# Where the fourth layer's modulation tiles are computed, and in which order the halved layers begin

## The reference, cut to what matters

```
sh1, sc1, gt1, sh2, sc2, gt2 = split(silu(c) @ w_ada[l] + b_ada[l], 6)     # for c and for c_ctx
h = rmsnorm(x, g2[l]) * (1 + sc2) + sh2
a, b = split(h @ w_up[l], 2)                                              # 2816 features each
x = x + gt2 * ((silu(a) * b) @ w_down[l])                                 # layers 0 and 1
x = x + gt2 * ((silu(dwconv3(a)) * b) @ w_down[l])                        # layers 2 and 3
```

## Time and profile before

| | |
|---|---|
| median of 3 runs | 3387.64 us (3385.45 to 3387.78) |
| the profiled execution's own time | 3385.83 us |
| its span | 3384.5 us |
| PE busy | 3247.7 us, 96% |
| VectorE (DVE) busy | 2159.3 us, 64% |
| FFN of layer 0, 1, 2, 3, about | 455 to 950, 1515 to 1862, 2218 to 2740, 2995 to 3375 us |

### The profile page before, as it was taken

One profiled execution on the slowest core, in us unless ns is written; L12 is line 12 of the kernel. 1 busy time (PEld: TensorE's weight loads), 2 busy tenths in 40 slices (PEclk: granted clock), 3 DMA queues, 4 the chain that ended last, 5 costly groups with the idle time before them and its releaser, 6 DMA issues. The chain is left out here.

```text
span 3384.5 us, 45127 instructions
## 1 busy us (share of the span) xinstructions
PE 3247.7 (96%) x17822; PEld 2767.8 (82%) x17822; DVE 2159.3 (64%) x3582; ACT 1404.8 (42%) x2261; POOL 223.0 (7%) x336
## 2 busy tenths in 40 slices
PE   6998999999999999999999999989999999999998
PEld 4787789999978888878888886889888987678887
DVE  4677477888765554558657466487888855654444
ACT  4567363333444334342223345363333443542333
POOL 0001100000010000003001000100000010010001
PEclk9999999999999999999999999999999999999999
DMA  5500123444221221215544211123444231123232
GB/s 216 216 23 2 38 77 123 132 143 137 87 90 50 96 77 50 90 69 195 173 148 156 84 45 51 44 86 116 140 127 129 87 99 57 44 83 99 90 101 83
DMA packets 98689, 334.39 MB, mean 99 GB/s; under 512 B 11872, under 2 KB 16768, under 8 KB 95024
## 3 DMA queue, kind: packets, MB, share of 16 engines
q1 hardware_dynamic: 77072, 252.63, 22.2%
q0 software_dynamic: 21408, 78.88, 7.4%
HBM read 329.37 MB, written 2.10 MB: 98 GB/s over the span
## 5 line engine op out<-in xcount | busy, mean ns | idle before, releaser
L1184 ACT ACTIVATE WH<-WR 128x1024 fp32r<-128x1024 f32 (+3 forms) x520 | 445.8, 859 | 1019.4 <-PE PS L586 749.1
L1797 DVE TENSOR_TENSOR WL<-WR,WH 128x1024 fp32r<-128x1024 f32 (+3 forms) x520 | 509.6, 981 | 478.6 <-ACT WH L1184 476.8
L586 PE MATMUL PS<-HH,WH 128*128 128x512 f32 (+1 forms) x1544 | 526.7, 373 | 10.7 <-DVE WL L1797 8.4
L586 PE MATMUL PS<-HH,WL 128*128 128x512 f32 (+1 forms) x1544 | 522.0, 370 | 0.0
L586 PE MATMUL PS<-HL,WH 128*128 128x512 f32 (+1 forms) x1544 | 521.7, 370 | 0.0
L586 PE MATMUL PS<-D,WH 128*128 128x512 f32 x1648 | 421.4, 361 | 0.3 <-DVE D L2244 0.2
L586 PEld LDWEIGHTS PS<-HH,WH 128*128 128x128 f32 x1544 | 270.0, 188 | 71.3 <-DVE WL L1797 12.9
L586 PEld LDWEIGHTS PS<-D,WH 128*128 128x128 f32 x1648 | 275.5, 188 | 52.5 <-DVE D L2244 2.0
L586 PEld LDWEIGHTS PS<-HL,WH 128*128 128x128 f32 x1544 | 268.9, 188 | 51.0 <-issue 1.0
L586 PEld LDWEIGHTS PS<-HH,WL 128*128 128x128 f32 x1544 | 269.2, 188 | 50.6
L586 PE MATMUL PS<-D,WL 128*128 128x512 f32 (+1 forms) x824 | 257.2, 360 | 0.0
(11 more groups left out here) (369 smaller groups left out, 6100.6 us busy)
## 6 DMA issues: line engine op xcount, KB each, us to landing
WR<-in_win SPq DMA_DIRECT2D x176, 512.0 KB, 3.5
AT<-in_adat POOLq DMA_DIRECT2D x144, 512.0 KB, 3.9
WR<-in_wret SPq DMA_DIRECT2D x64, 512.0 KB, 3.7
WR<-in_zin SPq DMA_DIRECT2D x36, 512.0 KB, 3.5
WR<-in_wdn SPq DMA_DIRECT2D x32, 448.0 KB, 3.4
WR<-in_wdn SPq DMA_DIRECT2D x48, 256.0 KB, 2.9
WR<-in_wdn SPq DMA_DIRECT2D x32, 320.0 KB, 2.9
AR<-in_ada SPq DMA_DIRECT2D x8, 1024.0 KB, 9.7
```

The source lines that it names most:

```text
L586: mm = PE.matmul(dst[:, a:b], w(u)[:, k * P:(k + 1) * P], h[:, k, a:b], start=(k == 0 and i == 0), stop=(k == nk - 1 and i == 2))
L1184: AC.activation(M.hi(u), M.raw(u), COPY).then_inc(*on.up("w_hi", u))
L1797: VE.tensor_tensor(M.lo(u), M.raw(u), M.hi(u).bitcast(F32), ALU.subtract).then_inc(*on.up("w_lo", u))
```

## The change

1. Tiles. The slots are now given by the FFN f in which they lie. FFN 1 gets the 48 tiles of layer 2 and the first 32 tiles of layer 3 (16 wide, 16 narrow). In its first two chunks a pair carries three tiles (the last pair of the chunk two) and each down product one; in the third chunk a pair carries three tiles, one wide and two narrow ones, and a down product none. All 48 of layer 2's tiles are of two instructions each. FFN 2 keeps 16 narrow tiles, all of them beside down products. In FFN 0 the two tiles of pairs 3 and 4 both stand beside pair 4.
2. Begin of the halved layers. The second sum of activation blocks has a place of its own (X2, where CB and the sums of weights lie), so `turned_low(1)` no longer has to follow `turned(3)`. On ACT `turned_high(0)` goes ahead of the refill of the fourth unit and `turned_high(3)` one half product later. On DVE `turned(3)`, `turned_low(0)`, `turned_low(3)` and the sums 7 and 3 of weights go behind the first refills of halves.
3. The convolution's steps in layer 2's halves. `conv_high` and `conv_low` of a pair go to the step behind product 1 of the pair after the next, and in the chunk's last pair behind product 2; `conv_multiply` goes from the step behind product 2 to the one behind product 5.

```diff
+EARLY = [(3, v) for v in range(32)]
+MORE = (6, 6, 8)
...
+        self.top = wide
+        self.X2 = t("X2", [P, 4, Q])
...
+def ada_slots(f):
     at = {}
+    wide, narrow = [(f + 1, v) for v in range(2 * KT)], [(f + 1, v) for v in range(2 * KT, NV)]
+    if f == 1:
+        wide = iter(wide + EARLY[:2 * KT])
+        narrow = iter(narrow + EARLY[2 * KT:])
+        for ch, nj in enumerate(CHUNKS[f]):
             for j in range(nj):
+                at["up", ch, j] = (next(wide), *(next(narrow) for _ in range(1 + (j < MORE[ch]))))
+            for m in range(KT if ch < 2 else 0):
+                at["down", ch, m] = (next(wide) if m < 5 else next(narrow),)
         return at
+    if f == 2:
+        narrow = [t for t in wide + narrow if t not in EARLY]
+    wide, narrow = iter(wide), iter(narrow)
+    for ch, nj in enumerate(CHUNKS[f]):
+        for j in range(nj):
+            if f == 0:
+                n = (2 if j == 4 else 0) if ch == 0 else 1 + (ch < 4 and j in (1, 2))
+            else:
+                n = 0
...
@@ ScalarE, halves
+            if l > 0 and i == 1 and j > js[1]:
+                conv_high(j - 2)
             if i in (1, 5, 6) or i == 3 and l > 0:
                 keep(j, i)
+            if l > 0 and i == 2 and j == js[-1]:
+                conv_high(j - 1)
...
-            if ch == 0 and q == 1:
+            if ch == 0 and q == 2:
                 turned_high(l, 3)
...
-                if i == (4 if j == js[-1] else 5) and j > js[0]:
-                    conv_high(j - 1)
@@ ScalarE, feed_forward
                 if l in HALVED and jj == 0:
                     whole(f"{l}b", l, [(1, k) for k in range(0 if l < 2 else 4, KT)])
+                    turned_high(l, 0)
                 refill(W.after(u, 4 if l in HALVED and jj else 3))
...
                     turned_high(l, 1)
                     turned_high(l, 2)
-                    turned_high(l, 0)
@@ VectorE, halves
+            if l > 0 and i == 1 and j > js[1]:
+                conv_low(j - 2)
+            if l > 0 and i == 2 and j == js[-1]:
+                conv_low(j - 1)
...
+            if ch == 0 and q == 0:
+                turned_low(l, 0)
             if ch == 0 and q == 1:
+                turned(l, 3)
+            if ch == 0 and q == 3:
                 turned_low(l, 3)
...
-                if i == (4 if j == js[-1] else 5) and j > js[0]:
-                    conv_low(j - 1)
...
-                if i == 2 and j > js[0]:
+                if i == 5 and j > js[0]:
                     conv_multiply(j - 1)
-            if i == 1 and (ch or j > js[0]):
+            if i == 1:
                 weight_sum(up + 2 * j, 3)
@@ VectorE, feed_forward
-                if l in HALVED and jj == 1:
-                    turned_low(l, 2)
-                    turned_low(l, 0)
                 refill(W.after(u, 2))
                 if l in HALVED and jj == 1:
                     refill(W.after(u, 3))
+                    turned_low(l, 2)
+                    weight_sum(up + 4, 7)
...
                         turned(l, 1)
                         turned(l, 2)
-                        turned(l, 3)
...
                 if l in HALVED and jj == 0:
-                    for i in (5, 6, 7, 3):
-                        weight_sum(up + 4, i)
+                    weight_sum(up + 4, 5)
+                    weight_sum(up + 4, 6)
                     turned_low(l, 1)
@@ GpSimd
+        for n in range(len(ada_order(l))):
+            modulation(l, n)
```

More of the change, by code:

```diff
@@ L539, in ada_columns @@
     return (0, 1) if l in (0, 2) or v < 2 * KT else (0,)
-def ada_slots(l):
+def ada_slots(f):
     at = {}
-    if l - 1 not in HALVED:
-        v = 0
-        for ch, nj in enumerate(CHUNKS[l - 1]):
-            for j in range(nj):
[L550 to L554, removed]
-        return at
[L556 to L559, removed]
-        for m in range(0 if ch else 1, KT - 2 if ch < 4 else 0):
-            at["down", ch, m] = (next(wide if ch == 0 or m in (1, 3, 4, 5)[4 - WIDE_DOWN[ch]:] else narrow),)
-    return at
@@ new lines, in ada_slots @@
+    if f == 2:
[7 more added lines that the diff above has]
+                n = 0
+            tiles = tuple(t for t in (next(narrow, None) for _ in range(n)) if t)
+            if tiles:
+                at["up", ch, j] = tiles
+        for m in range(0 if ch else 1, KT - 2 if ch < 4 else 0):
+            if f == 0 and (ch == 0 or m in (1, 3, 4, 5)[4 - WIDE_DOWN[ch]:]):
+                at["down", ch, m] = (next(wide),)
+            else:
+                tile = next(narrow, None)
+                if tile:
+                    at["down", ch, m] = (tile,)
@@ L570, in tensor_program, with ada_order @@
+    return at
+def ada_order(f):
+    return list(sum(ada_slots(f).values(), ()))
 def tensor_program(PE, M, on, FIRST):
@@ L1327, in turned_high @@
         else:
[L1328 removed]
+            dst, src = M.XH[:, n], M.X2[:, :, :] if n == 1 else M.XF[:, n]
         AC.activation(dst, src, COPY).then_inc(*on.up("t_hi", (l, n)))
@@ L1818, in scales, with ada_tiles @@
         step(i, ("scl", l, part))
[L1820 to L1824, removed]
+    def ada_tiles(f, tiles):
+        order = ada_order(f)
+        for l, v in tiles:
+            n = order.index((l, v))
             AT, cols = M.AT[n % 2], ada_columns(l, v)
@@ L1827, in ada_tiles @@
             if n:
-                VE.wait_ge(*on("ada_taken", (l, order[n - 1])))
+                VE.wait_ge(*on("ada_taken", order[n - 1]))
             for j in cols:
@@ L1834, in ada_bias @@
     def ada_bias(l):
-        VE.wait_ge(*on("ada_taken", (l, ada_order(l)[-1])))
+        VE.wait_ge(*on("ada_taken", ada_order(l - 1)[-1]))
         for j in range(2):
@@ L2083, in halves @@
         js, order, segs = range(plain(l, ch), nj), halves_order(l, ch), segments(l)
-        slots = ada_slots(ada)
+        slots = ada_slots(l)
         def ahead(n):
@@ L2183, in halves @@
             if i == 1 and ("up", ch, j) in slots:
-                if ch == 0 and j == js[1]:
+                if ch == 0:
                     VE.wait_ge(*on("cb", ada))
-                ada_tiles(ada, slots["up", ch, j])
+                ada_tiles(l, slots["up", ch, j])
         j = js[-1]
@@ L2202, in feed_forward @@
         n = segs[-1][1]
-        slots = ada_slots(ada) if ada is not None else {}
+        slots = ada_slots(l) if ada is not None else {}
         for ch, nj in enumerate(CHUNKS[l]):
@@ L2269, in feed_forward @@
                 if ada is not None:
-                    ada_tiles(ada, slots.get(("down", ch, m), ()))
+                    ada_tiles(l, slots.get(("down", ch, m), ()))
                 if ada is not None and ch == LAST[l] and m == 0:
@@ L2702, in squares, with modulation @@
             done = event
-    def modulation(l, n):
-        order = ada_order(l)
+    def modulation(f, n):
+        order = ada_order(f)
         if n == 0:
-            PO.dma_start(flat(M.CB, 0, 2), dram["cb"][min(l // 2, 1)]).then_inc(*on.up("cb_load", l, 16))
-        if n >= NV:
-            return
+            PO.dma_start(flat(M.CB, 0, 2), dram["cb"][min((f + 1) // 2, 1)]).then_inc(*on.up("cb_load", f + 1, 16))
         if n > 1:
-            PO.wait_ge(*on("ada_taken", (l, order[n - 2])))
-        PO.dma_start(M.AT[n % 2][:, :], dram["adat"][l - 1, order[n]]).then_inc(*on.up(f"mod_load{n % 2}", (l, order[n]), 16))
+            PO.wait_ge(*on("ada_taken", order[n - 2]))
+        l, v = order[n]
+        PO.dma_start(M.AT[n % 2][:, :], dram["adat"][l - 1, v]).then_inc(*on.up(f"mod_load{n % 2}", (l, v), 16))
     def feed_forward(l):
         PO.wait_ge(*(on("t_lo", (l, 3)) if l in HALVED else on("h_lo", (f"{l}b", 1, KT - 1))))
-        for n in range(NV):
-            modulation(l + 1, n)
+        for n in range(len(ada_order(l))):
+            modulation(l, n)
     def context_square(k):
@@ L2756, in pool_program @@
     squares("1b", S)
-    for n in range(NV):
-        modulation(2, n)
+    for n in range(len(ada_order(1))):
+        modulation(1, n)
         if 8 <= n < 16:
```

16 lines of the change are left out of this document (7 added, 9 removed).

## The result

The changed kernel takes 3400.95 us (median of 5 runs, 3398.43 to 3403.05), the kernel before 3385.86 us beside it: a ratio of 1.0044 with a 95% interval of 1.0031 to 1.0057. It is slower by 15 us, and the forecast of 3385 with its range up to 3396 was wrong. The span of the profiled execution is 3397.1 us, 12.6 more than before: the three changed FFNs are 16.2 us longer in it, and the stages between them, where the change does nothing, came 3.6 shorter.

What follows compares the result with a forecast made beforehand. PE, busy for 96% of the span, was taken as the bound, leaving about 137 us of idle time to win. The terms -17.1 + 16.6 - 2.0 + 0.3 = -2.2 us gave 3385 us, range 3371 to 3396.

Steps and rivals of the forecast that it cites:

- FFN 2's chunks: Fewer tiles and moved convolution steps: 3.9 us won in each of three chunks, 4.5 last, 0.9 first; 17.1 us together.
- bound of 10: FFN 2: only 10 us won if the moved steps make ACT's keep of product 1 late in each pair.
- two late spots: Last pair of FFN 2's chunks: join 7 about 0.6 us late, and 1.4 us idle before the down products.
- the 2 beside POOL: FFN 1's first chunk: 2 us more lost because POOL's squares of the context slow DVE's tiles beside them.
- The pair's cycle of 11.9 us: FFN 1's first two chunks: AT's load and two buffers set 11.9 us per pair, 1.0 us more than PE's.
- bound of 6: FFN 1: if loads cost nothing a pair takes 11.15 us and FFN 1 loses 6 us.
- rival A: Faster: loads don't limit FFN 1, which loses 6 us, and the rest stands: 3375 us; chance 0.3.
- The begin: Begin of the halved layers: 2.0 us won in layer 0, 0.3 lost in layer 2.
- (a): Begin of halved layers: turned_high(0) ahead of ACT's fourth-unit refill loses 1.4 us in layer 2, 0.8 in layer 0.
- (b): Begin of layer 2: the refill for product 6 comes late on DVE, so PE idles for 4 us.
- (c): Begin of layer 2: turned_high(3) waits on ACT for turned(3); product 5 can begin at 2253.5 against 2253.8 now.
- Rival D: Mildly slower: FFN 2 wins only 10 us as last pairs keep stalls, FFN 1 loses 17: 3393 to 3396; chance 0.1.

Runs made afterwards that it cites:

- e5_mult: Changed kernel with conv_multiply alone back behind product 2 (behind 5 in a chunk's last pair); 3393.20 us, ratio 1.0020.
- e1_conv_back: Changed kernel with all three convolution steps back at their old places, tiles and begin as changed; 3390.33 us, ratio 1.0013.
- e13_conv_only: Kernel before with the three convolution steps alone moved to their new places; 3399.39 us, ratio 1.0038.
- e9_tiles: Kernel before with 27 tiles moved, begin and convolution steps at their old places; 3370.47 us, ratio 0.9951.
- e4_third: Changed kernel with a third AT load buffer in FFN 1; 3396.80 us, ratio 1.0032.
- e2_begin_only: Kernel before with the changed begin of the halved layers alone (one tile of FFN 0 a pair later); 3388.46 us, ratio 1.0009.
- e8_cb: Changed kernel with convolution steps back, 27 tiles moved instead of 32, and CB's load issued earlier; 3370.12 us, ratio 0.9952.
- e12_high0: As e8_cb, with turned_high(0) on ACT behind the refill of the fourth unit instead of ahead; 3369.13 us, ratio 0.9945.
- e6_27: Changed kernel with convolution steps back and 27 tiles moved instead of 32, first-chunk pairs of FFN 1 keeping two tiles; 3372.71 us, ratio 0.9958.
- e3_deal212: Changed kernel with FFN 1's 32 tiles dealt as 12 wide and 20 narrow, pairs of two, one and two instructions; 3388.97 us, ratio 1.0007.

## Why the prediction was wrong, point by point

**FFN 2's chunks: the step that failed.** The forecast took 17.1 us from them; with the begin, FFN 2 came out 0.4 us longer. The bound named for this, "10 if the moved steps make ACT's `keep` of product 1 late in each pair (it now waits for `conv_low` of two pairs before; by my walk it is 0.75 us early)", was set aside by a walk that began the last pair with the pairs before it on time. They are not: DVE reaches join 7 of the pair before 1.7 us after ACT's copy for it is done. The walk also left out how `conv_multiply`'s move, from behind product 2 to behind product 5, puts it behind join 7, a sum and a refill, so that `conv_high`, `conv_low` and the copy can only follow one after the other. In the trace the copy is late. PE waits 1.38 us for it, where the walk had it 0.75 us early. Even the bound of 10 was too mild, for it allowed 7 us for this cost: by the places of product 4, the first two chunks lost 1.7 us together (the begin in it), the third and the fourth won 1.06 each and the last lost 0.7. e5_mult shows that the multiply's place is the main cause (10.5 us of FFN 2 back), e1_conv_back that all three steps together cost 14.1 us, and e13_conv_only that they cost it with the tiles in place as well.

**The tiles' part of FFN 2 was right.** With 27 of them gone and nothing else (e9_tiles) FFN 2 falls by 17.1 us and a chunk by 4.2 (3.9 forecast). That the total hits the term exactly is luck: the forecast credited it to a version with the convolution's steps moved, two late spots of which it had priced in. Its own sign for this, "if FFN 2's chunks still lose over 4 us each, tiles weren't their cause", would have misled: a changed chunk still loses 4.8 of the 5.9 us, and e9_tiles shows that tiles were the cause and that the moved steps had taken their place. The two late spots named for the last pair were right too: 0.9 us before product 4, where 0.6 was expected, and 0.54 + 0.78 at the down products, where 1.4 was.

**FFN 1: right in the sum and by chunks, not in the shares of its causes.** 16.6 forecast, 17.0 measured. By the places of the same matmuls the first chunk, with the wait of its first down product, lost 11.0 us (10.3 forecast, with the 2 beside POOL), the second brought it to 17.0 (6.3 forecast, 6.0 measured), the third nothing. The pair's cycle of 11.9 us over the load was 11.88, and the loads landed in 3.8 us in the median, as before. By the rule of the Trainium skill, page "DMA: Bandwidth & Descriptors", section "Anatomy of one DMA", it would have been an estimated 3.2 us and some 7 us lost; the trace disagrees. e4_third shows that the loads did limit, but by 5.8 us, not by the 10.6 between the forecast and its bound of 6 "if loads cost nothing": with no load waited for, FFN 1 still loses 11.3. So rival A would have missed even with fast loads, and the hit of 16.6 is in part luck.

**The begin.** Layer 0 won 1.2 us in FFN 0 (2.0 forecast; 1.9 in e2_begin_only); that distance scatters by 1 to 1.5 us with the same code, so these can't be told apart. The waits in layer 2 came as walked, (a) 1.45 us, (b) 3.85 where 4 was said; (c) was 0.72 us there and 2.14 in layer 0, where about 2 was said. As forecast (0.3 us), little was won up to product 5: it came 45.66 us after the begin, 0.2 us earlier than before. The step left out is what else hangs on `turned_low(3)`: CB's load, on POOL's queue, then ACT's silu and the refills behind it. e2_begin_only puts the total in layer 2 at 4.7 us lost with the tiles in place, e1_conv_back against e9_tiles at 3.5 without; e8_cb gives 1.7 of it back, and e12_high0 another 1.2 by the place of `turned_high(0)`. In the changed kernel this loss is part of FFN 2's 0.4.

**The sum.** -17.1 and +0.3 for FFN 2 became +0.4; put into the forecast of 3385.4 that alone gives 3402.6, and 3400.95 was measured. Rival D named a loss of this size in FFN 2's last pairs (3393 to 3396) with a chance of 0.1, for another reason ("the last pairs keep their stalls") and with the bound of 10; the measured time lies beyond it. None of the others came.

## What to carry to other kernels

A step that is moved takes its whole chain with it: before counting what it frees, follow each buffer's last reader to the next writer (here multiply, high, low, copy, product), over two pairs and from a late start, since the pairs before may be late, as they were here. Look also at the queues that wait for a moved step without being in the diff; here POOL's load of CB. And when several edits go together, cost each against the kernel without the others: 27 tiles alone give 15 us. The whole change took them and as much again: against e9_tiles, five more tiles in FFN 1 with their deal cost 16 us, and the moved steps with the begin 17.5 in FFN 2.

## What the runs showed of the hardware

The granted clock does not follow the length of an idle time alone. After 2.18 us it stood at 0.52. In the changed kernel it stood at 0.57 after 3.85 us; after 2.14 us it stayed at 1.00 in layer 0 and stood at 0.55 in layer 2. The windows behind these three waits, at 2261, 487 and 2294 us, clock in the third last column:

```profile
2261.00:2264.00 3.00, 3.00 (x12) 3.00 (x11) 3.00 (x4) 0.41 (x1) 0.00 (x0) 0.57 0.00 0
...
487.00:490.00 3.00, 3.00 (x19) 3.00 (x19) 3.00 (x4) 0.49 (x1) 0.89 (x2) 1.00 0.11 44
...
2294.00:2297.00 3.00, 3.00 (x10) 3.00 (x11) 2.60 (x5) 1.99 (x5) 0.00 (x0) 0.55 0.00 0
```

Nor is it the same in two kernels at the same place. At FFN 2's begin PE waits 1.28 and about 0.35 us in both e6_27 and e8_cb, and then the clock stood at 0.50 in the one (first row) and at 1.00 in the other:

```profile
2208.00:2210.00 2.00, 2.00 (x6) 1.59 (x5) 2.00 (x4) 1.35 (x2) 0.00 (x0) 0.50 0.00 0
```

```profile
2209.00:2211.00 2.00, 2.00 (x11) 1.63 (x10) 2.00 (x4) 1.15 (x2) 0.00 (x0) 1.00 0.00 0
```

This alone makes FFN 2 1.1 us longer in e6_27.

In FFN 1 a wait of 2.25 us (e3_deal212, at 1591.07) was followed by this:

```profile
1591.00:1594.00 3.00, 2.93 (x9) 2.36 (x10) 2.90 (x6) 0.95 (x1) 0.53 (x1) 0.72 0.64 228
```

So PE ran at 1.2 of 2.4 GHz for part of that window, and a late down product cost more than its wait: 3.7 us for 2.25. What tells these cases apart was not tested.

Beside POOL's squares one instruction of a tile takes DVE longer. Here are two tiles' first instructions in e4_third, and POOL's step that runs beside the second (last row):

```profile
1549.70 1.23 DVE L1852 SCALAR_TENSOR_TENSOR PS<-AT,CB 128x1024 f32<-128x1024 f32 x1
...
1554.07 1.64 DVE L1852 SCALAR_TENSOR_TENSOR PS<-AT,CB 128x1024 f32<-128x1024 f32 x1
```

```profile
1554.70 1.59 POOL L2759 TENSOR_TENSOR WK<-WK,WK 128x256 f32<-128x256 f32 x1
```
